# A hybrid decoder step on one core: sample attention in 32-column tiles, and one residual add moved in the FFN loops

## The chip, the cores and the metric

The kernel runs on one core of a Trainium2 chip, in one launch. The metric is the device time of that launch in microseconds (us); lower is better. The time given is the median of several runs, and one further execution was taken by the hardware profiler.

## What is computed

The reference is one inference step of a two-layer decoder trunk. 1024 prompt tokens and 8 samples of 4 new tokens each (32 rows) share all weights. Layer 0 mixes tokens with a gated short convolution, layer 1 with stick-breaking attention; each layer ends with a convolutional FFN of width 2816. Cut to what matters here:

```python
def stick_breaking(q, k, v, q_pos, k_pos, bias):
    z = einsum('bqhd,bkhd->bhqk', q, k) / sqrt(HEAD_DIM) + bias
    mask = k_pos < q_pos
    log_keep = where(mask, log_sigmoid(-z), 0)
    after = cumsum(log_keep, reverse=True) - log_keep
    w = where(mask, exp(log_sigmoid(z) + after), 0)
    return einsum('bhqk,bkhd->bqhd', w, v)

def conv_ffn(h, prev, w_up, w_dw, b_dw, w_down):
    g, u = split(h @ w_up, 2)
    gc, st = causal_dwconv(g, prev, w_dw)
    return (silu(gc + b_dw) * u) @ w_down, st
```

A sample's keys are 256 cached ones (two pages of 128) and its own new ones. There are 16 heads of 64, so the model width of 1024 is eight chunks of 128 features, and a chunk holds two heads.

## The kernel before, in words

All activations stay in SBUF, features on partitions and the 1056 tokens along the free axis in three blocks of 352. The large products are float32 split in three passes (`three`, lines 472 to 478): high part of the weights by high part of the activations, high by low, low by high. SyncE (SP) loads one raw weight tile after the other, GpSimd (POOL) splits it in `w_hi` and `w_lo`, TensorE (PE) multiplies, ScalarE (ACT) and VectorE (DVE) take the results out of PSUM. The order on every engine is written out by hand with semaphores; there is no planner.

**The FFN loop.** The 22 hidden chunks are worked in 11 pairs. After a first pair, five loop trips of two pairs each follow in each of the two layers, so 20 groups in all. A group is four up projections (gate and up of two chunks, `up`, `linear`) and then eight down tiles for the pair before (`down`, line 552). The results alternate between two PSUM areas `out[0]` and `out[1]`; `full[s]` tells that an area holds a result, `taken[s]` that it may be written again. In `down`, tile f waits for the area that tile f-2 has left (line 567). A down tile is 18 matmuls. DVE's `ffn_chunk` (line 1266) takes the gate (L1272), convolves it, scales it (L1279), multiplies with the up result straight from PSUM (L1283), waits until ACT has written `a_hi` (L948, in the rows the helper's line L836), and subtracts to get `a_lo` (L1285). After the second chunk's subtraction come the eight adds of the down tiles to the residual `x` (`add_x`, L1293), the one of tile 0 first. PE needs this group's `a_lo` only in the next group's down tiles (`a_ready`, line 565).

**Sample attention** stands between the prompt's attention and the output projection `wo`. It works on four pairs of samples, bp = 0 to 3. The 128 rows of a pair's scores are 2 samples of 64 rows, and these are 16 heads of 4 tokens. `q_rows` holds the queries as a stationary operand: for feature chunk c only the 8 columns of its two heads are nonzero. The steps of a pair:

- `sample_scores` (PE, line 761): 8 chunks by 2 samples, each a matmul of 64 stationary columns by 256 keys (L770), then 8 matmuls of 128 columns by the 32 new keys (L775) and a bf16 mask matmul (L777).
- `sample_sigmoids` (ACT, line 1092), `sample_weigh` (DVE, L1475 and L1477).
- `sample_turn` (PE, L784 and L785) and `sample_copy` (DVE, L1481 and L1482) turn the weights.
- `sample_values` (PE, line 788): 2 matmuls of 128 columns by 512 for the new values (L796), then 2 halves by 2 pages by 2 samples of 64 columns by 512 (L804). All 1024 features are computed for every head, in two PSUM banks `o_s`; a head's own 64 are picked at the end.
- `sample_rows` (ACT, line 1098) copies 128x1024 out of PSUM; `sample_out` (PE, L814) turns it in 8 transposes; `sample_take` (DVE, L1493) picks the heads' parts in 16 copies of 64x8 into `mixed`.

PE's order is `sample_scores(bp+1)`, `sample_out(bp-1)`, `sample_turn(bp)`, `sample_values(bp)`. The cached pages come by DMA from SP (lines 415 to 434): K and V of pairs 0 and 1 are loaded during the prompt's attention. Then K of pair 2 is issued once pair 0 is scored (line 424), V of pair 2 once pair 0's values are done (line 430), then SP reads the page numbers of pair 3 (line 419) and issues its K, and V of pair 3 follows once pair 1's values are done. A K or V load of a pair is four transfers of 512 KB. ACT reloads `x` (line 1090, 8 transfers of 528 KB) as the stage begins.

Of the kernel before, what the change touches and what calls it, by code (L numbers as in the profile page):

```python
# [21 lines left out]
P = 128  # L22
D = 1024
# [141 lines left out]
def build(nc, x_in, weights, taps_sc, taps_ffn, state_sc, state_ffn, gains, bias_heads, bias_rows,  # L165
# [6 lines left out]
    with ctx:  # L172
# [87 lines left out]

        q_rows = [sb(f"q_rows{n}", [P, KC * (P + 2 * NT)]) for n in range(2)]
        v_new = sb("v_new", [NS, D])
        o_rows = sb("o_rows", [P, D])
        beta_s = [sb(f"beta_s{n}", [P, PAST + NS]) for n in range(2)]
        keep_s = [sb(f"keep_s{n}", [P, PAST + NS]) for n in range(2)]
        prod_s = sb("prod_s", [P, PAST + NS])
# [17 lines left out]

        turned = [out[0][:, 2, :], out[1][:, 2, :]]
        attended = out[0][:, 1, :]
        o_s = out[0][:, 0:2, :].rearrange("p a b -> p (a b)")

        def sem(name):
            return ctx.enter_context(nc.semaphore(name))  # L290
# [180 lines left out]
        def _(pe):  # L471
# [289 lines left out]
            def sample_scores(bp):  # L761

                pe.wait_ge(s_set, bp + 1)
                bank_s = out[1][:, bp % 2, :]
                for b in range(2):
                    pe.wait_ge(page_k_in[2 * (bp % 2) + b], (bp // 2 + 1) * 32)
                for c in range(KC):
                    for b in range(2):
                        slot, rows = 2 * (bp % 2) + b, slice(64 * b, 64 * b + 64)
                        nc.tensor.matmul(bank_s[rows, 0:PAST], q_rows[bp % 2][:, c * P + 64 * b:c * P + 64 * b + 64],  # L770
                                         page_k[slot][:, c, :, :].rearrange("p g t -> p (g t)"),
                                         start=c == 0, stop=c == KC - 1, skip_group_check=True)

                for c in range(KC):
                    nc.tensor.matmul(bank_s[:, PAST:PAST + NS], q_rows[bp % 2][:, c * P:(c + 1) * P], k_s[:, c, :],  # L775
                                     start=c == 0, stop=False, skip_group_check=True)
                nc.tensor.matmul(bank_s[:, PAST:PAST + NS], ident_b[:, :], new_b[:, bp, :], start=False,  # L777
                                 stop=True, skip_group_check=True).then_inc(s_scored, 1)

# [8 lines left out]
            def sample_values(bp):  # L788

                pe.wait_ge(s_wt, bp + 1)  # L790

                if bp:
                    pe.wait_ge(s_o_rows, bp)

                for half in range(2):
                    nc.tensor.matmul(out[0][:, half, :], w_ts[0:NS, PAGES, :], v_new[:, 512 * half:512 * half + 512],  # L796
                                     start=True, stop=False, skip_group_check=True)
                for b in range(2):
                    pe.wait_ge(page_v_in[2 * (bp % 2) + b], (bp // 2 + 1) * 32)
                for half in range(2):  # L800
                    for g in range(PAGES):
                        for b in range(2):
                            slot, rows = 2 * (bp % 2) + b, slice(64 * b, 64 * b + 64)
                            mm = nc.tensor.matmul(out[0][rows, half, :], w_ts[:, g, rows],  # L804
                                                  page_v[slot][:, g, 512 * half:512 * half + 512], start=False,
                                                  stop=g == PAGES - 1, skip_group_check=True)
                mm.then_inc(s_full, 1)

            def sample_out(bp):
                pe.wait_ge(s_o_rows, bp + 1)  # L810

                pe.wait_ge(s_out, bp + 1)
                for c in range(KC):
                    mm = nc.tensor.transpose(score[1][:, c * P:(c + 1) * P], o_rows[:, c * P:(c + 1) * P], ident[:, :])  # L814
                mm.then_inc(s_o_turned, 1)

            sample_scores(0)
# [16 lines left out]
        def _(act):  # L834
# [262 lines left out]

            def sample_rows(bp):
                act.wait_ge(s_full, bp + 3)
                act_op(o_rows[:, :], o_s).then_inc(s_o_rows, 1)  # L1100

            sample_sigmoids(0)
            for bp in range(NB // 2):
# [23 lines left out]
        def _(dve):  # L1127
# [135 lines left out]
                        last.then_inc(tapped, 1)  # L1263
                last.then_inc(convolved, 1)

            def ffn_chunk(m, par, chunk, layer, k, trip, slot):
# [12 lines left out]
                V.tensor_tensor(y[par][:, :], y[par][:, :], rstd[:, :], ALU.mult).then_inc(y_scaled, 1)  # L1279
                dve.wait_ge(y_scaled, m + 1)  # L1280
                dve.wait_ge(full[s], trip * TRIP_FILLS + (FULL[name][s] + (k + 1) // 2 + 1))
                yy = wide(y[par][:, :])
                V.tensor_tensor(yy, yy, result(s), ALU.mult).then_inc(taken[s], 1)  # L1283
                dve.wait_ge(a_high, m - (KC - 1))
                V.tensor_tensor(a_lo[:, slot, par, :], y[par][:, :], a_hi[:, slot, par, :].bitcast(f32),  # L1285
                                ALU.subtract).then_inc(a_ready, 1)
# [8 lines left out]
            def ffn(layer):  # L1295
                name = f"ffn{layer}"
                m0 = M_FFN[layer]

                def up(m, chunk, k0, trip, slot):
                    for p in range(2):  # L1300
                        ffn_chunk(m + p, p, chunk + p, layer, k0 + 2 * p, trip, slot)

                def down(k0, trip):
                    for f in range(KC):
                        add_x(f, name, k0 + f, trip)

                up(m0, 0, 0, 0, 0)
                with dve.Fori(0, FFN_TRIPS) as i:
                    for n in range(2):
                        k0 = (4 + KC) * n + 4  # L1310
                        up(i * 4 + (m0 + 2 + 2 * n), i * 4 + (2 + 2 * n), k0, i, (n + 1) % 2)
                        down(k0 + 4, i)

            dve.wait_ge(gain_loaded, 16)
# [169 lines left out]
            def sample_take(bp):  # L1484

                dve.wait_ge(s_o_turned, bp + 1)
                for h in range(2):
                    rows = slice(DH * h, DH * h + DH)
                    o = mixed[rows, :, SEQ + bp * 2 * NT:SEQ + (bp + 1) * 2 * NT].rearrange("p c (b t) -> p c b t", b=2)

                    r = score[1][rows, :].rearrange("p (c b r) -> p c b r", c=KC, b=2)
                    for c in range(KC):
                        last = V.tensor_copy(o[:, c, :, :], r[:, c, :, 8 * c + 4 * h:8 * c + 4 * h + NT])  # L1493
                last.then_inc(s_out, 1)

            sample_q(0)
# [126 lines left out]
```

## Time and profile before

| | us |
|---|---|
| median of 3 runs | 2708.8 |
| lowest and highest | 2707.02 and 2710.52 |
| the profiled execution, its own time | 2711.09 |
| its span, first to last instruction | 2709.3 |
| PE busy with matmuls | 2609.6 |
| DVE busy | 1475.8 |
| POOL busy | 725.2 |
| ACT busy | 539.9 |

The time of an execution is its span and 1.8 us around it. Two records of the profile stand for each float32 matmul that isn't a transpose, because PE makes two passes; so 16 matmuls are "x32". In a form such as "128*64 128x256" the first pair is rows by stationary columns of the array, and the second is what streams through. "PEld" is the loading of the stationary operand, which runs beside PE's matmuls. The column "idle before" gives how long an engine had nothing to do and what ended that.

### The profile page before, as it was taken

To read this page: it belongs to the slowest core of one execution; us is meant where nothing else is said; L and a number is where in the kernel's file an instruction comes from. 1 tells how busy PE (TensorE), PEld (TensorE's weight loads), DVE (VectorE), ACT (ScalarE), POOL (GpSimd) and SP (SyncE) were. 2 spreads that over 40 slices of the span, in tenths; PEclk is the share of its full clock that TensorE was granted. 3 is DMA by queue.
4 is the path that set the end of the run, shared out by engine and by line. 5 is a ranking of instruction groups with operands and counts; after the bars stand their busy time and mean duration, and the time that the engine had idled before them with its cause. 6 is when DMAs were issued, how large, how long until landed. Compare 5 with 4: busy or idle time off the path is not lost.

```text
span 2709.3 us, 40755 instructions
## 1 busy us (share of the span) xinstructions
PE 2609.6 (96%) x16774; PEld 2472.5 (91%) x16774; DVE 1475.8 (54%) x1512; ACT 539.9 (20%) x1077; POOL 725.2 (27%) x415
## 2 busy tenths in 40 slices
PE   7999999999999999989999999789999999999996
PEld 7999999999999999988888888459999999999995
DVE  7333455444444455587777777533754444444446
ACT  4000221000000000144444444320300000000013
POOL 3333333223332233221111111013322233333333
PEclk9999999999999999999999999899999999999998
DMA  4111111111111111121111111631111111111111
GB/s 137 47 42 45 48 47 40 47 47 47 43 44 47 47 47 40 50 111 40 40 40 40 44 44 40 220 102 47 39 40 47 47 47 47 47 47 47 47 42 65
DMA packets 60330, 149.04 MB, mean 55 GB/s; under 512 B 5522, under 2 KB 28818, under 8 KB 60178
## 3 DMA queue, kind: packets, MB, share of 16 engines
q1 hardware_dynamic: 51298, 123.86, 14.2%
q10 hardware_dynamic: 8880, 22.85, 2.2%
q8 instruction: 132, 2.16, 0.3%
q14 instruction: 20, 0.16, 0.0%
HBM read 128.91 MB, written 17.78 MB: 54 GB/s over the span
## 4 chain that ended last, share of the span: by engine, by line
PE 86%; DVE 8%; issue 2%; ACT 2%; POOL 1%; DMA 0%; SPq 0%; DVEq 0%; POOLq 0%; ACTq 0%
PE bank L474 26%; PE bank L478 25%; PE bank L477 25%; PE bank L706 3%; PE bank L646 3%; PE bank L679 2%; DVE a_lo L1285 1%; DVE h_lo L1155 1%; DVE total L1164 1%; DVE x L1293 1%; DVE y L1283 1%; ACT a_hi L836 1%; POOL y_rows L466 1%; PE bank L770 1%; PE bank L804 1%
## 5 line engine op out<-in xcount | busy, mean ns | idle before, releaser
L474 PE MATMUL bank<-h_hi,w_hi 128*128 128x352 f32 x3648 | 1197.1, 328 | 29.8 <-DVE ext L1272 8.8
L478 PE MATMUL bank<-h_hi,w_lo 128*128 128x352 f32 x3648 | 1177.6, 323 | 0.0
L477 PE MATMUL bank<-h_lo,w_hi 128*128 128x352 f32 x3648 | 1176.6, 323 | 0.0
L450 POOL CAST w_hi<-raw 128x1024 fp32r<-128x1024 f32 x196 | 217.9, 1112 | 1937.7 <-PE bank L474 1894.3
L474 PEld LDWEIGHTS bank<-h_hi,w_hi 128*128 128x128 f32 x3648 | 690.2, 189 | 42.5 <-issue 31.2
L477 PEld LDWEIGHTS bank<-h_lo,w_hi 128*128 128x128 f32 x3648 | 691.7, 190 | 0.7 <-issue 0.4
L478 PEld LDWEIGHTS bank<-h_hi,w_lo 128*128 128x128 f32 x3648 | 691.3, 190 | 0.0
L452 POOL TENSOR_TENSOR w_lo<-raw,w_hi 128x1024 fp32r<-128x1024 f32 x196 | 488.1, 2490 | 15.7
L1293 DVE TENSOR_TENSOR x<-x,bank 128x1056 f32<-128x1056 f32 x174 | 216.2, 1251 | 290.8 <-PE bank L478 290.8
L474 PE MATMUL bank<-a_hi,w_hi 128*128 128x352 f32 x1056 | 343.9, 326 | 11.7 <-DVE x L1293 11.7
L477 PE MATMUL bank<-a_lo,w_hi 128*128 128x352 f32 x1056 | 342.1, 324 | 0.0
L478 PE MATMUL bank<-a_hi,w_lo 128*128 128x352 f32 x1056 | 341.1, 323 | 0.0
L1272 DVE TENSOR_TENSOR ext<-bank,rstd 128x1056 f32<-128x1056 f32 x44 | 55.4, 1259 | 333.7 <-PE bank L478 333.6
L474 PEld LDWEIGHTS bank<-a_hi,w_hi 128*128 128x128 f32 x1056 | 198.7, 188 | 20.1 <-DVE x L1293 16.3
L1405 DVE TENSOR_TENSOR_SCAN prod<-keep 128x895 f32<-128x895 f32 (+7 forms) x128 | 196.5, 1535 | 21.5 <-ACT keep L836 17.1
L836 ACT ACTIVATE smp<-ext 128x32 f32<-128x32 f32 x52 | 12.0, 231 | 949.3 <-DVE ext L1272 858.9
L477 PEld LDWEIGHTS bank<-a_lo,w_hi 128*128 128x128 f32 x1056 | 198.2, 188 | 0.2
L478 PEld LDWEIGHTS bank<-a_hi,w_lo 128*128 128x128 f32 x1056 | 198.3, 188 | 0.0
L836 ACT ACTIVATE beta<-bank,bias_pair 128x896 f32<-128x896 f32 (+7 forms) x128 | 94.9, 741 | 222.6 <-PE bank L649 218.6
L1285 DVE TENSOR_TENSOR a_lo<-y,a_hi 128x1056 fp32r<-128x1056 f32 x44 | 105.4, 2396 | 52.4 <-ACT a_hi L836 52.4
L1409 DVE TENSOR_TENSOR beta<-beta,prod 128x895 f32<-128x895 f32 (+7 forms) x128 | 125.3, 979 | 4.4
L1247 DVE TENSOR_SCALAR y<-ext,tap_ffn 128x1024 f32<-128x1024 f32 x44 | 116.3, 2643 | 9.7 <-DVE ext L1272 9.6
(111 smaller groups left out, 1757.7 us busy)
## 6 DMA issues: line engine op xcount, KB each, us to landing
raw<-weights SPq DMA_DIRECT2D x196, 512.0 KB, 3.4
page_k<-cache_k SPq DMA_DIRECT2D x16, 512.0 KB, 7.0
page_v<-cache_v SPq DMA_DIRECT2D x16, 512.0 KB, 6.1
x_spill<-x ACTq DMA_DIRECT2D x8, 528.0 KB, 6.1
k_out<-k_t ACTq DMA_DIRECT2D x8, 528.0 KB, 2.7
v_out<-v_t ACTq DMA_DIRECT2D x8, 528.0 KB, 2.9
x<-x_spill ACTq DMA_DIRECT2D x8, 528.0 KB, 7.4
y_out<-y_rows ACTq DMA_DIRECT2D x3, 1408.0 KB, 5.3
```

The source lines that it names most:

```text
L450: nc.gpsimd.tensor_copy(w_hi[ring][:, :], raw[slot][:, :]).then_inc(w_high, 1)
L452: nc.gpsimd.tensor_tensor(w_lo[ring][:, :], raw[slot][:, :], w_hi[ring][:, :].bitcast(f32), ALU.subtract).then_inc(w_split, 1)
L474: mm = nc.tensor.matmul(o, w_hi[w][:, c0:c0 + P], hi, start=first, stop=False)
L477: nc.tensor.matmul(o, w_hi[w][:, c0:c0 + P], lo, start=False, stop=False)
L478: return nc.tensor.matmul(o, w_lo[w][:, c0:c0 + P], hi, start=False, stop=last)
L646: nc.tensor.matmul(score[h][:, n0:n1], q_t[par][rows, i * P:(i + 1) * P], k_t[par][rows, n0:n1], start=True, stop=n1 < width)
L836: return nc.scalar.activation(o, i, func, **kw)
L1247: V.tensor_scalar(o[:, 0:SEQ], e[:, 0:SEQ], tap(0), None, ALU.mult).then_inc(tapped, 1)
L1285: V.tensor_tensor(a_lo[:, slot, par, :], y[par][:, :], a_hi[:, slot, par, :].bitcast(f32), ALU.subtract).then_inc(a_ready, 1)
L1293: V.tensor_tensor(xx, xx, result(s), ALU.add).then_inc(taken[s], 1)
L1405: V.tensor_tensor_scan(prod[:, width - 1:0:-1], back, back, 1.0, ALU.mult, ALU.bypass).then_inc(scanned, 1)
L1409: V.tensor_tensor(w[:, 0:width - 1], w[:, 0:width - 1], prod[:, 1:width], ALU.mult).then_inc(weighed, 1)
```

## The change

It has two parts. In sample attention the stationary operands shrink to 32 columns: each of the four quarters of the score rows (a sample's heads 0 to 7 or 8 to 15) takes only the four chunks that can be nonzero for it, and only its own half of the features of V. The output per pair is then 128x512 in one bank, so `o_rows` and `o_s` are two half-size buffers used in turn, the transposes go from 8 to 4 (into `spare`, one bank for each parity), and the picking copies from 16 of 64x8 to 8 of 64x16. The waits follow: values of bp wait for the row copy of bp-2, the row copy of bp for the transposes of bp-2, the transposes of bp for the picking of bp-2. In the FFN loops the add of down tile 0 moves ahead of the second chunk's last subtraction.

```diff
-        o_rows = sb("o_rows", [P, D])
+        o_rows = [sb(f"o_rows{n}", [P, D // 2]) for n in range(2)]
-        o_s = out[0][:, 0:2, :].rearrange("p a b -> p (a b)")
+        o_s = [out[0][:, n, :] for n in range(2)]
+        o_turned = [spare[:, n, :] for n in range(2)]
...
-                for c in range(KC):
+                for cc in range(KC // 2):
                     for b in range(2):
-                        slot, rows = 2 * (bp % 2) + b, slice(64 * b, 64 * b + 64)
-                        nc.tensor.matmul(bank_s[rows, 0:PAST], q_rows[bp % 2][:, c * P + 64 * b:c * P + 64 * b + 64],
-                                         page_k[slot][:, c, :, :].rearrange("p g t -> p (g t)"),
-                                         start=c == 0, stop=c == KC - 1, skip_group_check=True)
-
-                for c in range(KC):
-                    nc.tensor.matmul(bank_s[:, PAST:PAST + NS], q_rows[bp % 2][:, c * P:(c + 1) * P], k_s[:, c, :],
-                                     start=c == 0, stop=False, skip_group_check=True)
+                        for g in range(2):
+                            c, r = cc + g * KC // 2, 64 * b + 32 * g
+                            nc.tensor.matmul(bank_s[r:r + 32, 0:PAST], q_rows[bp % 2][:, c * P + r:c * P + r + 32],
+                                             page_k[2 * (bp % 2) + b][:, c, :, :].rearrange("p g t -> p (g t)"),
+                                             start=cc == 0, stop=cc == KC // 2 - 1, skip_group_check=True)
+
+                for cc in range(KC // 2):
+                    for b in range(2):
+                        for g in range(2):
+                            c, r = cc + g * KC // 2, 64 * b + 32 * g
+                            nc.tensor.matmul(bank_s[r:r + 32, PAST:PAST + NS], q_rows[bp % 2][:, c * P + r:c * P + r + 32],
+                                             k_s[:, c, :], start=cc == 0, stop=False, skip_group_check=True)
...
-                if bp:
-                    pe.wait_ge(s_o_rows, bp)
-
-                for half in range(2):
-                    nc.tensor.matmul(out[0][:, half, :], w_ts[0:NS, PAGES, :], v_new[:, 512 * half:512 * half + 512],
-                                     start=True, stop=False, skip_group_check=True)
+                if bp >= 2:
+                    pe.wait_ge(s_o_rows, bp - 1)
+
+                for r in range(0, P, 32):
+                    g = r // 32 % 2
+                    nc.tensor.matmul(o_s[bp % 2][r:r + 32, :], w_ts[0:NS, PAGES, r:r + 32],
+                                     v_new[:, 512 * g:512 * g + 512], start=True, stop=False, skip_group_check=True)
...
-                for half in range(2):
-                    for g in range(PAGES):
-                        for b in range(2):
+                for page in range(PAGES):
+                    for r in range(0, P, 32):
+                        b, g = r // 64, r // 32 % 2
+                        mm = nc.tensor.matmul(o_s[bp % 2][r:r + 32, :], w_ts[:, page, r:r + 32],
+                                              page_v[2 * (bp % 2) + b][:, page, 512 * g:512 * g + 512], start=False,
+                                              stop=page == PAGES - 1, skip_group_check=True)
...
-                pe.wait_ge(s_out, bp + 1)
-                for c in range(KC):
-                    mm = nc.tensor.transpose(score[1][:, c * P:(c + 1) * P], o_rows[:, c * P:(c + 1) * P], ident[:, :])
+                pe.wait_ge(s_out, max(bp, 1))
+                for cc in range(KC // 2):
+                    mm = nc.tensor.transpose(o_turned[bp % 2][:, cc * P:(cc + 1) * P],
+                                             o_rows[bp % 2][:, cc * P:(cc + 1) * P], ident[:, :])
...
                 act.wait_ge(s_full, bp + 3)
-                act_op(o_rows[:, :], o_s).then_inc(s_o_rows, 1)
+                if bp >= 2:
+                    act.wait_ge(s_o_turned, bp - 1)
+                act_op(o_rows[bp % 2][:, :], o_s[bp % 2]).then_inc(s_o_rows, 1)
...
                 V.tensor_tensor(yy, yy, result(s), ALU.mult).then_inc(taken[s], 1)
+                if between is not None:
+                    between()
                 dve.wait_ge(a_high, m - (KC - 1))
...
                 def down(k0, trip):
-                    for f in range(KC):
+                    for f in range(1, KC):
                         add_x(f, name, k0 + f, trip)
...
-                        up(i * 4 + (m0 + 2 + 2 * n), i * 4 + (2 + 2 * n), k0, i, (n + 1) % 2)
+                        up(i * 4 + (m0 + 2 + 2 * n), i * 4 + (2 + 2 * n), k0, i, (n + 1) % 2,
+                           lambda: add_x(0, name, k0 + 4, i))
                         down(k0 + 4, i)
...
-                    for c in range(KC):
-                        last = V.tensor_copy(o[:, c, :, :], r[:, c, :, 8 * c + 4 * h:8 * c + 4 * h + NT])
+                    for c in range(KC // 2):
+                        last = V.tensor_copy(o[:, c, :, :, :], r[:, c, :, :, 8 * c + 4 * h:8 * c + 4 * h + NT])
```

`between` runs for the second chunk of a group only (`between if p else None`).

## Rows read from the trace of the kernel before

**Rows 1.** The page: span, busy time of the engines, chain that ended last.

```profile
span 2709.3 us, 40755 instructions
...
PE 2609.6 (96%) x16774; PEld 2472.5 (91%) x16774; DVE 1475.8 (54%) x1512; ACT 539.9 (20%) x1077; POOL 725.2 (27%) x415
...
PE 86%; DVE 8%; issue 2%; ACT 2%; POOL 1%; DMA 0%; SPq 0%; DVEq 0%; POOLq 0%; ACTq 0%
```

**Rows 2.** Waits of PE, 425 to 1145 us (layer 0's FFN): total us, times, longest.

```profile
PE bank L474 <- DVE x L1293: 4.3, 10, 0.4
```

**Rows 3.** Waits of PE, 1930 to 2660 us (layer 1's FFN).

```profile
PE bank L474 <- DVE x L1293: 5.8, 11, 1.5
```

**Rows 4.** Timeline of DVE, 2005 to 2012 us: start, us, instructions, idle before.

```profile
2005.46 1.25 DVE L1283 TENSOR_TENSOR y<-y,bank 128x1056 f32<-128x1056 f32 x1 [1.63 <-PE bank L478]
2007.87 2.52 DVE L1285 TENSOR_TENSOR a_lo<-y,a_hi 128x1056 fp32r<-128x1056 f32 x1 [1.16 <-ACT a_hi L836]
2010.31 2.40 DVE L1293 TENSOR_TENSOR x<-x,bank 128x1056 f32<-128x1056 f32 x2
```

**Rows 5.** Timeline of PE, 2010.5 to 2011.7 us.

```profile
2010.70 0.32 PE L477 MATMUL bank<-a_lo,w_hi 128*128 128x352 f32 x1
2010.86 0.32 PE L478 MATMUL bank<-a_hi,w_lo 128*128 128x352 f32 x1
2011.61 0.43 PE L474 MATMUL bank<-a_hi,w_hi 128*128 128x352 f32 x1 [0.42 <-DVE x L1293]
```

**Rows 6.** Timeline of PE, 1740 to 1809.2 us (sample attention).

```profile
1740.95 5.50 PE L770 MATMUL bank<-page_k,q_rows 128*64 128x256 f32 x32 [0.31 <-DVE q_rows L1465]
...
1763.67 3.62 PE L770 MATMUL bank<-page_k,q_rows 128*64 128x256 f32 x32
1767.22 1.97 PE L775 MATMUL bank<-k_s,q_rows 128*128 128x32 f32 x16
...
1771.16 1.98 PE L796 MATMUL bank<-v_new,w_ts 32*128 32x512 f32 x4 [0.70 <-DVE w_ts L1482]
1773.07 3.65 PE L804 MATMUL bank<-page_v,w_ts 128*64 128x512 f32 x16
1778.85 5.33 PE L770 MATMUL bank<-page_k,q_rows 128*64 128x256 f32 x32 [2.12 <-DMA page_k<-cache_k]
...
1785.95 1.07 PE L814 MATMUL bank<-ident,o_rows 128*128 128x128 f32 x8
...
1798.77 5.35 PE L804 MATMUL bank<-page_v,w_ts 128*64 128x512 f32 x16
...
1809.11 0.40 PE L474 MATMUL bank<-h_hi,w_hi 128*128 128x352 f32 x1 [2.78 <-DVE h_lo L1241]
```

**Rows 7.** Timeline of PE's weight loads, 1732.8 to 1734.3 us (prompt attention).

```profile
1732.84 0.64 PEld L706 LDWEIGHTS bank<-w_first,v_rows 128*64 128x64 f32 x12 [1.58 <-ACT w_first L836]
```

**Rows 8.** Windows of sample attention; last three columns: granted clock, DMA share, GB/s.

```profile
1740.00:1757.50 17.50, 16.49 (x108) 10.51 (x106) 5.77 (x14) 1.78 (x4) 0.00 (x0) 0.79 1.05 352
1753.70:1763.90 10.20, 9.50 (x30) 3.15 (x31) 2.12 (x6) 0.90 (x3) 0.00 (x0) 0.67 0.45 112
1763.90:1783.80 19.90, 17.07 (x111) 9.94 (x108) 3.45 (x22) 2.93 (x4) 0.00 (x0) 0.91 0.97 316
```

**Rows 9.** Timeline of SP's DMA issues, 1690 to 1830 us.

```profile
1763.89 1.78 SPq L433 DMA_DIRECT2D page_v<-cache_v  x4
1768.53 4.82 SPq L427 DMA_DIRECT2D page_k<-cache_k  x4
1776.77 1.77 SPq L433 DMA_DIRECT2D page_v<-cache_v  x4
```

**Rows 10.** Timeline of ACT, 1755 to 1809 us (the row copies).

```profile
1804.16 1.02 ACT L836 ACTIVATE o_rows<-bank 128x1024 f32<-128x1024 f32 x1 [9.48 <-PE bank L804]
```

**Rows 11.** Groups of ACT, 1690 to 1740 us: busy us, mean ns, idle before.

```profile
L836 ACT ACTIVATE mixed<-bank 128x512 f32<-128x512 f32 x3 | 1.8, 602 | 5.0 <-PE bank L706 5.0
```

**Rows 12.** Timeline of DVE, 1803 to 1808 us (the picking copies).

```profile
1806.37 1.43 DVE L1493 COPY mixed<-bank 64x8 f32<-64x8 f32 x16 [8.22 <-PE bank L814]
```

More of the change, by code:

```diff
@@ L790, in sample_values @@
                 pe.wait_ge(s_wt, bp + 1)
-                if bp:
-                    pe.wait_ge(s_o_rows, bp)
-                for half in range(2):
-                    nc.tensor.matmul(out[0][:, half, :], w_ts[0:NS, PAGES, :], v_new[:, 512 * half:512 * half + 512],
-                                     start=True, stop=False, skip_group_check=True)
+                if bp >= 2:
[4 more added lines that the diff above has]
+                                     v_new[:, 512 * g:512 * g + 512], start=True, stop=False, skip_group_check=True)
                 for b in range(2):
                     pe.wait_ge(page_v_in[2 * (bp % 2) + b], (bp // 2 + 1) * 32)
-                for half in range(2):
-                    for g in range(PAGES):
-                        for b in range(2):
[L803 to L806, printed above, removed]
+                for page in range(PAGES):
[4 more added lines that the diff above has]
+                                              stop=page == PAGES - 1, skip_group_check=True)
                 mm.then_inc(s_full, 1)
@@ L1264, in conv, with ffn_chunk @@
                 last.then_inc(convolved, 1)
-            def ffn_chunk(m, par, chunk, layer, k, trip, slot):
+            def ffn_chunk(m, par, chunk, layer, k, trip, slot, between=None):
                 name = f"ffn{layer}"
@@ L1297, in ffn, with up @@
                 m0 = M_FFN[layer]
-                def up(m, chunk, k0, trip, slot):
+                def up(m, chunk, k0, trip, slot, between=None):
                     for p in range(2):
-                        ffn_chunk(m + p, p, chunk + p, layer, k0 + 2 * p, trip, slot)
+                        ffn_chunk(m + p, p, chunk + p, layer, k0 + 2 * p, trip, slot, between if p else None)
                 def down(k0, trip):
-                    for f in range(KC):
+                    for f in range(1, KC):
                         add_x(f, name, k0 + f, trip)
@@ L1488, in sample_take @@
                     rows = slice(DH * h, DH * h + DH)
-                    o = mixed[rows, :, SEQ + bp * 2 * NT:SEQ + (bp + 1) * 2 * NT].rearrange("p c (b t) -> p c b t", b=2)
-                    r = score[1][rows, :].rearrange("p (c b r) -> p c b r", c=KC, b=2)
-                    for c in range(KC):
-                        last = V.tensor_copy(o[:, c, :, :], r[:, c, :, 8 * c + 4 * h:8 * c + 4 * h + NT])
+                    o = mixed[rows, :, SEQ + bp * 2 * NT:SEQ + (bp + 1) * 2 * NT].rearrange("p (g c) (b t) -> p c b g t", g=2, b=2)
+                    r = o_turned[bp % 2][rows, :].rearrange("p (c b g r) -> p c b g r", c=KC // 2, b=2, g=2)
+                    for c in range(KC // 2):
+                        last = V.tensor_copy(o[:, c, :, :, :], r[:, c, :, :, 8 * c + 4 * h:8 * c + 4 * h + NT])
                 last.then_inc(s_out, 1)
```

## The prediction, made before the changed kernel was run

> **What bounds the kernel now.** I read the page first: PE is busy for 96% of the span and carries 86% of the chain that ended last [rows 1]. So only what shortens PE's stream, or a wait in it, can count. The waits of PE over each layer's FFN come next: 10 waits for the residual add in one layer and 11 in the other, all but one at most 0.4 us long [rows 2, 3]. There are 10 groups a layer, so every group of the FFN loop has one. The timelines of DVE and PE around one show why. The last up tile ends at 2005.4; DVE multiplies, waits for ACT, subtracts until 2010.3, and only then adds down tile 0, until 2011.56 [rows 4]. PE starts a matmul every 0.16 us, but after the one at 2010.86 the next starts at 2011.61 [rows 5]: down tile 2 needs the area that this add sets free.
>
> The third reading is PE's timeline of sample attention, from the first score matmul at 1740.95 to the first matmul of `wo` at 1809.11, 68.2 us [rows 6]. PE is not the only bound there. For pair 3 it waits 2.1 us for pages [rows 6], and the windows show the DMA engines saturated from 1740 to 1757.5 (share 1.05, 352 GB/s), and nearly so from 1763.9 to 1783.8 (0.97, 316 GB/s) [rows 8]. The same matmuls also take longer in places: 32 records of L770 took 5.50 and 5.33 us at two places and 3.62 at a third, and 16 of L804 took 5.35 instead of 3.65 [rows 6]. From 1753.7 to 1763.9 the granted clock was 0.67 [rows 8], a mixture of 1.2 and 2.4 GHz, after PE had waited for the turned weights.
>
> **The FFN part.** Nothing is added or removed; one add of 1.25 us (2.40 for two) passes one subtraction of 2.5 us [rows 4]. The stall costs 0.75 - 0.16 = 0.59 us [rows 5], and 20 x 0.59 = **11.8 us**. What is late next? A down tile is 18 matmuls of 0.16, 2.9 us. In the example group tile 0 ends at 2005.4 + 2.9 = 2008.3. DVE's wait for it now stands ahead of the subtraction; DVE had been idle until 2007.87 anyway [rows 4]. The add ends at 2009.6, well before tile 2 is due at 2011.2; the subtraction ends at 2012.1, the add of tile 1 at 2013.4, and tile 3 is due at 2014.1. So 0.7 us is left. Queued behind the moved wait are only DVE's own subtraction and adds; PE needs `a_lo` in the next group, four up tiles later. No DMA issue or other queue is passed. Bounds: 11.8 if the cover holds; were each group 0.7 + 0.2 us later, 20 x 0.2 = 4 us of it would come back. I take 11.8.
>
> **The sample part, PE's work for a pair.** Matmuls of 64 columns in different halves of the array already overlap: 32 records of 256 columns take 3.55 us to the next line's start, 0.22 for two [rows 6], and 512 columns take 3.70 us for 16 records, 0.46 for two (to the issue at 1776.77 that their end releases [rows 6, 9]). If four quarters overlap as two halves do:
> - L770: still 32 records, now four at a time, 8 x 0.22 = 1.8 us, down 1.8.
> - L775: 16 records of 128 columns take 1.8 us (0.11 each); 32 records of 32 columns replace them. No row has such loads in a stream. The nearest is the 12 loads of 64 columns in 0.64 us, 0.05 each [rows 7], which gives 32 x 0.05 = 1.7. I take no change; the bounds are half of it (-0.9) and one 0.11 for each (+1.8).
> - L796: 4 records in turn take 1.91 us [rows 6]; 8, four at a time, 0.95.
> - L804: 16 records, four at a time, 4 x 0.46 = 1.85, down 1.85. The values together go from 5.6 to 2.8.
> - L814: 4 transposes instead of 8 in 1.07 [rows 6], down 0.45. The row copy halves, 1.02 [rows 10] to the 0.60 of a 128x512 copy [rows 11]. Picking: 8 copies instead of 16 in 1.43, 0.09 each [rows 12], down 0.7; doubling 8 columns to 16 is costed at nothing.
>
> L770's new form needs a weight load and a matmul every 0.22 / 4 = 0.055 us, just what rows 7 show, so that is where it may fall short. The new waits reach back two pairs, and what they wait for ended a whole pair ago; they cost nothing.
>
> **Where it stays on the path.** Most of the saved time of pairs 0 to 2 meets the page loads.
> - K of pair 2 shares saturated engines with the reload of `x`; an earlier issue doesn't bring its end ahead of 1757.5 [rows 8]. The scores of pair 2 started at 1763.67 [rows 6]. By the terms above pairs 0 and 1 are scored by about 1750 and values(0) ends at 1754 (at full clock) to 1757 (at half). So PE waits here, up to 3 us.
> - V of pair 2 is then issued at about 1755.5 instead of 1763.89 [rows 9]. K of pair 3 is issued 4.6 us behind it (1768.53 [rows 9]), and landed 15.0 behind it (1778.85 [rows 6]): 1770.5. By the rate, from 1757.5 on 4.2 MB at 316 GB/s [rows 8] end at 1770.8. I take 1770.8, between 1769 and 1772: **8.0 us** earlier than before.
> - From there PE's chain runs to the end, and V of pair 3 is in by about 1777, ahead of its use. Scores(3) start after a wait and were slow before (7.1 us from 1778.85 to 1785.95 [rows 6]); with half the clock for four quarters 3.6 + 1.8, down 1.7. Then two rounds of values: 2.8 for pair 2, and 3.0 for pair 3, where 5.35 [rows 6] shows the lower clock (I take a mixture again). Three rounds of transposes, 3 x 0.45; two row copies, 2 x 0.4; the last picking, 0.7. Together 1.7 + 2.8 + 3.0 + 1.35 + 0.8 + 0.7 = **10.3 us**.
>
> Sum: 8.0 + 10.3 = 18.3 for the stage, with 11.8 for the FFNs 30.1 us. The profiled execution took 2711.09 us, so it would take 2681.0; that execution lies 2.3 above the median of 2708.8, so the median forecast is **2678.7 us**. The bounds of the stage: if every round after K of pair 3 runs at the lower clock and the pages land at 1772, the gain is 18.3 - 2.8 - 1.3 - 1.2 = 13; if all run at the upper, pages land at 1769 and L775 halves, 18.3 + 1.8 + 1.3 + 0.9 = 22. I give the forecast 2674 to 2684.
>
> The Trainium skill ("TensorE: Matmul & The Clock Gate", section on packing small matmuls) puts three column tiles at 2.38 times one, not 3 times. By that, an estimate, a group of four would take 1.26 times a single one, some 2 us more over the last chain, and the time would be near 2681. The same skill ("TensorEngine Tiling (Array Packing)", Instruction Overhead) warns against tiling where a dimension is already small, which speaks against the new L775 with its 32 streamed columns; no run here shows its charge yet.
>
> **The rivals.**
> 1. *Quarters overlap only two at a time*, or loads and issue hold L770 to 0.11 us a record as L775's loads do. For: no row shows four. Against: two halves overlap in full. Then scores and values keep their length, L775 costs up to 1.8 more, and of the stage only the transposes, copies and picking stay, about 3 us, less about one L775 round of 1.8: 2708.8 - 11.8 - 1 = **2696**. Chance 0.13.
> 2. *Quarters run one after another* (the slower side). The place is PE's L770, L796 and L804: (32 x 0.22) + (24 x 0.46) = 18.1 us a pair against 9.2, plus 8.9 - 0.85 = 8.0, four times 32; the page waits give about 3 back, the FFN part 11.8. That is 2708.8 + 17 = **2726**. It decides below about 1.3 quarters at a time, where the stage's loss passes 11.8. Against it stand the overlapping halves. Chance 0.04.
> 3. *The FFN stall only moves*: the subtraction now stands behind the add, and tile 3 waits for the add of tile 1. For: only 0.7 us of cover, and the subtraction's length depends on POOL's work beside it. Against: it would need nearly 1 us more. Price: 4 to 12 us back, **2687** in the middle. Chance 0.06.
> 4. *The page loads take back more*: with PE idle twice, pair after pair runs at the lower clock, and the stage gives 11 instead of 18: **2686**. Chance 0.09.
>
> **The chances.** The forecast has 0.68; the rivals 0.13, 0.04, 0.06 and 0.09. The range holds forecast, rivals 3 and 4 and the optimistic end: 2673 to 2692, 0.83 in all. A measurement of this kernel tells 0.2% (5.4 us) from no change. Only rival 2 is slower: slower 0.05; same 0.03, for two rivals meeting; faster 0.92.
>
> **What would show it.** In the changed profile: no wait of PE for L1293 in the 20 groups, DVE's order multiply, add, subtract; 32 records of L770 in about 1.9 us at full clock and 16 of L804 in 1.9; scores(2) starting near 1757.5 and scores(3) near 1771, both released by pages; the first matmul of `wo` near 1791. If L770 still takes 3.6 us, quarters don't overlap and the sum for the stage falls; if the stage ends near 1791 but the total doesn't follow, the FFN part is wrong.

## The result, and the profile after

The changed kernel takes 2683.9 us (median of 4 runs, 2680.5 to 2688.8) against 2707.9 for the kernel before (4 runs): a ratio of 0.991, 95% interval 0.989 to 0.993, so 24.0 us less. The forecast was 2678.7, 29 us less than the same median. The profiled execution took 2683.9 us, 27.2 less than that of before.

The page of the changed kernel, its first lines and its chain of waits:

```profile
span 2682.1 us, 40852 instructions
...
PE 2582.4 (96%) x16838; PEld 2461.6 (92%) x16838; DVE 1450.8 (54%) x1480; ACT 537.9 (20%) x1077; POOL 724.8 (27%) x415
...
PE 90%; DVE 5%; issue 2%; ACT 1%; SPq 1%; POOL 1%; DMA 1%; POOLq 0%; DVEq 0%; ACTq 0%
```

PE's share of the chain rose from 86 to 90% and DVE's fell from 8 to 5% [rows 1]: the 20 pieces of the chain that ran through a multiply, ACT's copy, a subtraction and an add are gone. PE's waits from 425 to 1150 us, layer 0's FFN:

```profile
PE bank L475 <- DVE x L1303: 1.5, 1, 1.5
```

and DVE's timeline in a group of layer 1:

```profile
1983.03 1.25 DVE L1291 TENSOR_TENSOR y<-y,bank 128x1056 f32<-128x1056 f32 x1 [1.70 <-PE bank L479]
1985.91 1.25 DVE L1303 TENSOR_TENSOR x<-x,bank 128x1056 f32<-128x1056 f32 x1 [1.62 <-PE bank L479]
1987.08 1.25 DVE L1295 TENSOR_TENSOR a_lo<-y,a_hi 128x1056 fp32r<-128x1056 f32 x1
1988.79 1.25 DVE L1303 TENSOR_TENSOR x<-x,bank 128x1056 f32<-128x1056 f32 x1 [0.46 <-PE bank L479]
```

The ten waits of [rows 2] are gone; the one that is left is the 1.5 us one outside the groups, which [rows 3] had too. The order is as forecast: multiply, add, subtract, add. The subtraction takes 1.25 us in its new place, not the 2.5 of [rows 4], so DVE is ahead of its work: it stands idle for 0.46 us before the add of tile 1.

PE's timeline of sample attention, which answers to [rows 6]:

```profile
1735.84 3.34 PE L772 MATMUL bank<-page_k,q_rows 128*32 128x256 f32 x32 [1.14 <-DVE q_rows L1476]
1739.01 0.48 PE L780 MATMUL bank<-k_s,q_rows 128*32 128x32 f32 x32
1739.54 1.93 PE L772 MATMUL bank<-page_k,q_rows 128*32 128x256 f32 x32
...
1743.20 1.06 PE L802 MATMUL bank<-v_new,w_ts 32*32 32x512 f32 x8 [0.70 <-DVE w_ts L1493]
1744.19 1.92 PE L809 MATMUL bank<-page_v,w_ts 128*32 128x512 f32 x16
1754.65 3.64 PE L772 MATMUL bank<-page_k,q_rows 128*32 128x256 f32 x32 [8.54 <-DMA page_k<-cache_k]
...
1767.00 3.64 PE L772 MATMUL bank<-page_k,q_rows 128*32 128x256 f32 x32 [3.48 <-DMA page_k<-cache_k]
...
1779.83 3.53 PE L809 MATMUL bank<-page_v,w_ts 128*32 128x512 f32 x16
1784.09 0.66 PE L819 MATMUL bank<-ident,o_rows 128*128 128x128 f32 x4 [0.73 <-ACT o_rows L842]
1786.95 0.63 PE L475 MATMUL bank<-h_hi,w_hi 128*128 128x352 f32 x1 [2.21 <-DVE h_lo L1249]
```

Four quarters stream at a time without loss: 32 records of L772 in 1.93 us where two halves took 3.62, and 16 of L809 in 1.92 instead of 3.65. The new keys (L780) fell from 1.97 to 0.48. From the first score matmul to the first of `wo` the stage takes 1786.95 - 1735.84 = 51.1 us, where it took 68.2. And PE now waits 12.0 us for pages, 8.5 and 3.5, where it waited 2.1. SP's issues show what the loads do now:

```profile
1739.80 9.37 SPq L428 DMA_DIRECT2D page_k<-cache_k  x4
1749.26 3.10 SPq L434 DMA_DIRECT2D page_v<-cache_v  x4
1755.28 6.69 SPq L428 DMA_DIRECT2D page_k<-cache_k  x4
```

The columns of the table are worked from the timelines of the profiled executions, in us. "K2" and "K3" are the starts of the scores of pairs 2 and 3 after the first score matmul; "FFN 1 to end" runs from the first matmul of `wo` to the end of the span.

| kernel | K2 | K3 | stage | FFN 1 to end |
|---|---|---|---|---|
| before | 22.7 | 37.9 | 68.2 | 900.2 |
| changed | 18.8 | 31.2 | 51.1 | 895.1 |
| forecast | 16.6 | 29.9 | 49.9 | |
| e1_ffn_only | 19.0 | 33.9 | 64.2 | 896.1 |
| e2_sample_only | 18.4 | 31.2 | 51.2 | 901.3 |
| e3_quarters_in_turn | 18.0 | 31.3 | 52.6 | 897.5 |
| e7_before_x_late | 19.1 | 33.9 | 64.2 | 899.9 |
| e4_x_late | 14.5 | 27.6 | 44.6 | 895.1 |
| e5_k_first | 19.0 | 27.6 | 43.2 | 894.1 |
| e6_both | 14.8 | 24.0 | 41.3 | 894.6 |
| e9_order_filled | 15.4 | 22.8 | 38.7 | 895.3 |
| e11_v_after_k | 18.5 | 33.2 | 50.7 | 895.8 |

### The profile page after: what moved, and what is told of

It is laid out like the page before. It is cut to its first block, busy times and chain, and to the rows that moved or that the text cites. A ratio compares the mean times of both kernels' runs of the same rounds, so it can differ in the third digit from the quotient of the medians.

```text
span 2682.1 us, 40852 instructions
## 1 busy us (share of the span) xinstructions
PE 2582.4 (96%) x16838; PEld 2461.6 (92%) x16838; DVE 1450.8 (54%) x1480; ACT 537.9 (20%) x1077; POOL 724.8 (27%) x415
## 4 chain that ended last, share of the span: by engine, by line
PE 90%; DVE 5%; issue 2%; ACT 1%; SPq 1%; POOL 1%; DMA 1%; POOLq 0%; DVEq 0%; ACTq 0%
PE bank L475 27%; PE bank L479 27%; PE bank L478 27%; PE bank L707 3%; PE bank L647 3%; PE bank L680 2%; DVE total L1172 1%; DVE h_lo L1163 1%; POOL y_rows L467 1%; SPq L428 1%; PE bank L650 0%; DVE h_lo L1249 0%; DVE x L1221 0%; DMA x<-x_in 0%; ACT beta L842 0%
## 5 line engine op out<-in xcount | busy, mean ns | idle before, releaser
L453 POOL TENSOR_TENSOR w_lo<-raw,w_hi 128x1024 fp32r<-128x1024 f32 x196 | 488.3, 2491 | 15.7
L1262 DVE SCALAR_TENSOR_TENSOR y<-ext,tap_ffn,y 128x1024 f32<-128x1024 f32 x88 | 113.0, 1284 | 0.0
```

Source lines behind the costliest of these rows:

```text
L453: nc.gpsimd.tensor_tensor(w_lo[ring][:, :], raw[slot][:, :], w_hi[ring][:, :].bitcast(f32), ALU.subtract).then_inc(w_split, 1)
L1262: main = V.scalar_tensor_tensor(o[:, 0:SEQ], e[:, n:n + SEQ], tap(n), o[:, 0:SEQ], ALU.mult, ALU.add)
```

## The experiments

Each ratio below is against runs of the kernel before made beside that experiment. Differences to the changed kernel are differences of medians from different rounds, so where they are small the intervals of the ratios and the lengths of the stage say more.

**One part at a time.** First the kernel before with the moved add alone; the edit is the FFN part of the diff above.

> The kernel before with the moved add alone. Theory (20 stalls of 0.59 us go, nothing takes their place): 11.8 us less than before, near 2696, PE waits for the residual add only once or twice in the FFN loops. Rival (the stall moves to down tile 3, or PE waits elsewhere): 0 to 8 us less. In the changed kernel's trace the two FFN loops gave back about 6.3 and 5.0 us, so 10 to 12 is expected.

Measured: 2696.1 us, ratio 0.996 (0.995 to 0.998), 12.3 us less than the kernel before. Its waits of PE from 425 to 2650 us have one line for the residual add:

```profile
PE bank L474 <- DVE x L1295: 3.1, 2, 1.5
```

Twice 1.5 us, one in each layer's FFN and both outside the groups. The stall went and nothing took its place.

Then the other part alone:

```diff
-                    for f in range(1, KC):
+                    for f in range(KC):
...
-                        up(i * 4 + (m0 + 2 + 2 * n), i * 4 + (2 + 2 * n), k0, i, (n + 1) % 2,
-                           lambda: add_x(0, name, k0 + 4, i))
+                        up(i * 4 + (m0 + 2 + 2 * n), i * 4 + (2 + 2 * n), k0, i, (n + 1) % 2)
```

> The changed kernel with the residual adds in their old place: the sample part alone. Theory (the two parts lie in different stretches and add up): the stage takes 51 us instead of 68, so 17 us less than before, near 2691, and 20 stalls of PE on the residual add are back. Rival (the parts are not additive, or the stage's length depends on how the run falls): 12 to 14 us less, which with 11.8 for the other part would give the 24 that were measured for both.

Measured: 2694.9 us, ratio 0.995 (0.994 to 0.996), 13.5 us less. Its waits of PE over the same stretch:

```profile
PE bank L772 <- DMA page_k<-cache_k: 11.8, 2, 8.1
PE bank L475 <- DVE x L1303: 11.6, 22, 1.5
```

The 20 stalls are back. 12.3 and 13.5 make 25.8, and both together gave 24.0, within the scatter of these medians: the parts add up. But the sample part is worth 13.5 us, not 17 (my expectation) nor 18.3 (the forecast), although the stage takes 51.2 us in this trace as in the changed kernel's. The table has the reason. The stage of before took 68.2 us in the one execution that I had, and 64.2 in the two others with the same stage, e1_ffn_only and e7_before_x_late. PE's timeline of e1_ffn_only:

```profile
1750.28 3.65 PE L804 MATMUL bank<-page_v,w_ts 128*64 128x512 f32 x16
...
1768.64 3.67 PE L770 MATMUL bank<-page_k,q_rows 128*64 128x256 f32 x32 [1.82 <-DMA page_k<-cache_k]
```

For the first of these two places [rows 8] had a clock of 0.67, and the trace of before has there:

```profile
1754.97 3.77 PE L796 MATMUL bank<-v_new,w_ts 32*128 32x512 f32 x4 [0.70 <-DVE w_ts L1482]
1758.67 5.17 PE L804 MATMUL bank<-page_v,w_ts 128*64 128x512 f32 x16
```

This is where most of the 4 us lie: the scores of pair 2 start at 22.7 there and at 19.0 here. The second place, 5.33 us in [rows 6], makes no difference in the sum, since e1_ffn_only pays as much at the values of pair 2; from the scores of pair 3 to `wo` both traces take 30.3 us. Whether PE falls to 1.2 GHz at a given place differs between executions of the same stage, and mine was a slow one. 64.2 - 51.2 = 13.0 is what this part is worth against the other two executions: 2.7 us from the earlier scores of pair 3 (33.9 and 31.2) and 10.3 from what follows them (30.3 and 20.0).

**Do quarters need neighbours?** The loops of the scores, new keys and cached values were swapped, so that one quarter's matmuls come in a row:

```diff
-                for cc in range(KC // 2):
-                    for b in range(2):
-                        for g in range(2):
+                for b in range(2):
+                    for g in range(2):
+                        for cc in range(KC // 2):
...
-                for page in range(PAGES):
-                    for r in range(0, P, 32):
+                for r in range(0, P, 32):
+                    for page in range(PAGES):
```

> The changed kernel with the same matmuls, but all of one quarter of the columns before the next quarter's (scores, new keys, cached values). Theory (the gain is that four quarters stream at a time, and this needs neighbours in different quarters): 32 score records take about 32 x 0.21 = 6.8 us instead of 1.75, the 16 of the cached values 6.8 instead of 1.8, together some 10 us more for each pair, 30 us or more over the stage after the page waits give some back: 2710 to 2720. Rival (the gain is only that columns of zeros are dropped, or the engine overlaps quarters over any distance): within 4 us of the changed kernel.

Measured: 2688.8 us, ratio 0.992 (0.991 to 0.994), 5 us more than the changed kernel by the medians, with overlapping intervals, and not 30; the stage is 1.5 us longer. PE's timeline of this kernel from 1745.7 to 1754.8 us:

```profile
1745.78 3.95 PE L772 MATMUL bank<-page_k,q_rows 128*32 128x256 f32 x29
1749.35 0.40 PE L780 MATMUL bank<-k_s,q_rows 128*32 128x32 f32 x8
1749.56 0.38 PE L772 MATMUL bank<-page_k,q_rows 128*32 128x256 f32 x1
1749.56 0.41 PE L780 MATMUL bank<-k_s,q_rows 128*32 128x32 f32 x12
1749.78 0.38 PE L772 MATMUL bank<-page_k,q_rows 128*32 128x256 f32 x1
...
1752.81 1.94 PE L809 MATMUL bank<-page_v,w_ts 128*32 128x512 f32 x16
```

The cached values, 4 records in a row for each quarter, overlap in full (1.94). The scores, 8 in a row, overlap in part: 3.57 us to the first new key where neighbours take 1.75. New-key records start ahead of the last score records, though the program has them behind: quarters run on independently, over some distance. The Trainium skill says that matmuls start and end in program order ("TensorE: Matmul & The Clock Gate", section on packing small matmuls); the starts in this trace are not in that order. So neither theory held. The expectation's 30 us fell, and the rival's "over any distance" did too. From the first score record to the end of the new keys PE lost 2.6 us a pair (for pair 1, 4.8 us instead of 2.2), and for the pairs ahead of the page loads the wait took it back: 2.60 us of wait before pair 2 instead of 8.54.

**The pages.** What bounds the stage now? The reload of `x` moved from ACT at the stage's start to SP, behind the last page:

```diff
-            for f in range(KC):
-                act.dma_start(x[:, f, :], x_spill[f, :, :]).then_inc(x_back, 16)
...
+            sp.wait_ge(x_spilled, 16 * KC)
+            for f in range(KC):
+                sp.dma_start(x[:, f, :], x_spill[f, :, :]).then_inc(x_back, 16)
             rest = N_TILES - early
```

> The changed kernel with the reload of x (4.3 MB) issued by SP after the last pages, instead of by ACT at the stage's start. Theory (K of pair 2 came 18.8 us after the first score matmul because it shared the DMA engines with x): K of pair 2 lands about 7 us earlier, and K of pair 3 with it by 4 to 7 us; x is back before the first tile of the output projection is added: 4 to 7 us less than the changed kernel, near 2678. Rival (the page loads are slow by themselves, through their small pieces or SP's issue): no change.

Measured: 2678.8 us, ratio 0.989 (0.988 to 0.991), 5.1 less than the changed kernel, though the intervals overlap; the stage takes 44.6 us instead of 51.1. K of pair 2 came 4.4 us earlier, K of pair 3 3.5, and the chain behind it took 17.0 us instead of 20.0, for a reason that the part on the clock gives. The same edit on the kernel before:

> The kernel before with the late reload of x. Theory (the pages came in time before, but for about 2 us, and became the bound only through the faster matmuls): at most 2 us less than before, 2706 to 2709. Rival (the share that x takes of the DMA engines held up the kernel before too): 4 us less or more.

Measured: 2706.7 us, ratio 0.9997 (0.9987 to 1.0007). Nothing, and its stage takes 64.2 us as in e1_ffn_only. So the bound by page loads is one that the faster matmuls uncovered.

Then the order of SP's issues, K of pair 3 ahead of V of pair 2, with the page numbers read first; the loop is unrolled, and its second half becomes:

```diff
+            ids2, ids3 = pages_of(2), pages_of(3)
+            load_k(2, ids2)
+            load_k(3, ids3)
+            load_v(2, ids2)
+            load_v(3, ids3)
```

> The changed kernel with K of pair 3 issued before V of pair 2, and the page numbers of both read ahead of the waits (PE needs this K first). Theory (the stage hangs on the landing of K of pair 3, 31.2 us after the first score matmul, because its issue stands behind V of pair 2 in SP's queue): K of pair 3 lands near 27 us, V of pair 2 then becomes the wait at 33: 2 to 4 us less than the changed kernel, 2680 to 2682. Rival (only the bytes count, the order doesn't): no change.

Measured: 2675.2 us, ratio 0.987 (0.986 to 0.989), 8.7 less than the changed kernel, more than the 2 to 4 that I expected: V of pair 2 did not become the wait. All that PE waits for in this stage:

```profile
PE bank L780 <- DMA page_k<-cache_k: 8.8, 1, 8.8
PE bank L810 <- DVE w_ts L1501: 2.8, 4, 0.7
PE bank L483 <- DVE h_lo L1257: 2.2, 1, 2.2
PE bank L827 <- ACT o_rows L850: 1.4, 2, 0.7
PE bank L780 <- DVE q_rows L1484: 1.2, 1, 1.2
```

K of pair 3 is there when PE comes for it. The stage is 7.9 us shorter than the changed kernel's (43.2 and 51.1). Only 3.6 of them are the earlier start of the scores of pair 3. The other 4.3 lie behind it: with no wait before these scores, PE's chain to `wo` takes 15.7 us instead of 20.0. The window of this kernel over the beginning of that chain has the full clock, with the DMA engines as busy as in the changed kernel (columns as in [rows 8]):

```profile
1765.00:1770.00 5.00, 4.30 (x80) 2.10 (x76) 2.50 (x12) 0.89 (x2) 0.00 (x0) 1.00 0.99 384
```

Both edits together:

> The order of e5_k_first together with the late reload of x of e4_x_late. Theory (page loads are the bound, x takes a share of the DMA engines, and the order puts the wrong load first): K of pair 2 lands 14.5 us after the first score matmul, K of pair 3 near 20, V near 26 and 32, the stage takes 38 to 40 us instead of 44.6 in e4_x_late: near 2673. Rival (PE's own chain and its low clock after waits bound the stage by now): 42 to 44 us, 2676 to 2679.

Measured: 2671.9 us, ratio 0.986 (0.985 to 0.988). The stage of the profiled execution takes 41.3 us, between the theory and the rival; that execution, at 2677.6, was the slowest of its four.

**When did K of pair 2 land?** The forecast had it 16.6 us after the first score matmul, and it was 18.8.

```diff
                     sp.wait_ge(s_full, i * 2 + (pair + 1))
+                    for n in (2 * pair, 2 * pair + 1):
+                        sp.wait_ge(page_k_in[n], i * 32 + 32)
```

> The changed kernel, V of each pair issued only when K of the same pair has landed. Theory (K of pair 2 landed 2.2 us later than forecast because V of pair 2 was by then issued early enough to take a share of the DMA engines): K of pair 2 lands 16.5 to 17 us after the first score matmul instead of 18.8; K of pair 3 is issued later, so the stage is no shorter: 2683 to 2687. Rival (K of pair 2 is slow through the reload of x alone): it still lands at 18.8, and the stage grows by 2 us or more.

Measured: 2684.4 us, ratio 0.991 (0.989 to 0.992), as the changed kernel; K of pair 2 still let PE go only at 18.5, so my theory fell. The windows of this kernel show what I had misread:

```profile
1752.40:1754.40 2.00, 0.00 (x0) 0.00 (x0) 0.00 (x0) 0.00 (x0) 0.00 (x0) 0.53 1.18 287
1754.40:1756.40 2.00, 0.00 (x0) 0.00 (x0) 0.00 (x0) 0.00 (x0) 0.00 (x0) 0.50 0.95 234
1756.40:1757.80 1.40, 0.00 (x0) 0.00 (x0) 0.00 (x0) 0.00 (x0) 0.00 (x0) 0.50 0.05 14
```

The first score matmul is at 1739.3 here. The bulk of the bytes is through by 1756.4, 17.1 us after it and near the forecast's 16.6, but PE starts at 1757.84. A trickle of small packets runs on behind the bulk (the 0.05 of the last window), and the last of the four transfers, issued at 1750.6, lands 7.1 us later, at 1757.7: PE starts 0.1 us behind that. The trace of before had the same tail. There the last transfer of K of pair 2 was issued at 1752.1 and landed 7.4 us later, at 1759.5, which is 18.5 us after the first score matmul and 2.0 us after the 1757.5 at which the forecast had it. Nothing waited for it there, so it stood in no list of waits. The rival's rise of the stage by 2 us didn't come either; K of pair 3 came 2.0 later, and PE's chain behind it took 17.5 us instead of 20.0, its last values at the full clock (1.92 us instead of 3.53).

**The clock after a wait.** PE's waits for pages were filled with matmuls that feed nothing:

```diff
+                for n in range({2: 16, 3: 7}.get(bp, 0)):
+                    nc.tensor.matmul(out[0][0:P, 2, 0:512], ident[:, :], mixed[:, n % KC, 0:512],
+                                     start=True, stop=True, skip_group_check=True)
                 for b in range(2):
                     pe.wait_ge(page_k_in[2 * (bp % 2) + b], (bp // 2 + 1) * 32)
```

> The changed kernel with 16 and 7 float32 matmuls of 128 columns by 512 that feed nothing, placed where PE waits for K of pairs 2 and 3 (6.8 and 3.0 us of work at the full clock, in waits of 8.5 and 3.5). Theory (scores, transposes and new keys of pairs 2 and 3 take twice as long because the clock falls while PE waits): scores of both pairs take 1.9 us instead of 3.6 and the stage ends 2 to 4 us earlier; only what follows K of pair 3 counts: near 2681. Rival (the clock falls for another reason, or the filling delays the real work by as much): no change or up to 3 us more.

Measured: 2687.8 us, ratio 0.992 (0.991 to 0.993). I had sized the filling wrong: a float32 matmul is two records, so 16 took not 6.8 but 14.0 us. The timeline of PE:

```profile
1745.98 14.00 PE L767 MATMUL bank<-mixed,ident 128*128 128x512 f32 x32
...
1772.82 1.93 PE L775 MATMUL bank<-page_k,q_rows 128*32 128x256 f32 x32
...
1788.51 0.40 PE L475 MATMUL bank<-h_hi,w_hi 128*128 128x352 f32 x1 [2.21 <-DVE h_lo L1252]
```

It overran both waits, and the stage grew by only 2 us, because the chain from the scores of pair 3 to `wo` now took 1788.51 - 1772.82 = 15.7 us where it took 1786.95 - 1767.00 = 20.0. The windows of the two kernels over their chains show the clock. Kernel with the filling:

```profile
1772.80:1788.50 15.70, 10.66 (x132) 4.43 (x132) 5.47 (x34) 3.34 (x8) 0.00 (x0) 1.00 0.04 17
```

and the changed kernel, its wait for K of pair 2, the scores behind it, the scores of pair 3, and the last values:

```profile
1746.10:1754.60 8.50, 0.01 (x2) 0.00 (x0) 0.00 (x0) 0.60 (x1) 0.00 (x0) 0.67 1.14 316
1754.60:1758.60 4.00, 3.95 (x64) 2.40 (x64) 0.00 (x0) 0.00 (x0) 0.00 (x0) 0.50 1.02 394
...
1767.00:1771.00 4.00, 4.00 (x64) 2.31 (x65) 0.00 (x0) 0.00 (x0) 0.00 (x0) 0.50 0.98 363
1778.80:1783.50 4.70, 4.56 (x24) 0.75 (x24) 0.72 (x8) 0.06 (x1) 0.00 (x0) 0.64 0.00 0
```

So 4.3 us of the changed kernel's chain hang on the clock. The DMA engines were idle over the chain of e8_filled and not in the changed kernel; that they aren't the cause is shown by e5_k_first, whose chain took the same 15.7 us beside page loads. A filling of the right length was to collect them, 9 and 3 matmuls instead of 16 and 7:

> The changed kernel with 9 and 3 matmuls that feed nothing (7.7 and 2.6 us) in PE's waits of 8.5 and 3.5 us for K of pairs 2 and 3, in place of the 14.0 and 6.3 us of e8_filled, which overran them. Theory (clock): from the landing of K of pair 3 to the output projection PE's chain took 20.0 us in the changed kernel and 15.7 in e8_filled; with the filling inside the waits the stage ends about 4 us earlier, near 2680. Rival: the filling delays K of pair 3 or its scores, no change.

Measured: 2681.9 us, ratio 0.989 (0.988 to 0.991), 2 less than the changed kernel, with overlapping intervals. In the profiled execution K of pair 3 came late, at 32.1 us, PE stood idle for 4.0 us behind the filling, and the scores took 3.64 us again. So this is inconclusive.

On top of e6_both, 4 such matmuls before the scores of pair 2 (the same edit with other numbers), and then 2 more before `wo`:

> The kernel of e6_both with 4 matmuls that feed nothing (0.85 us each at the full clock, as e8_filled showed: 16 took 14.0) in PE's 4.3 us wait for K of pair 2. Theory (what is left of the stage is PE's chain, and half of it runs at the lower clock after this wait): scores of pair 2 take 1.9 us instead of 3.6 and what follows is faster too, 3 to 5 us less than e6_both, near 2668. Rival (the chain is bound by the waits between engines, not by the clock): within 1 us of e6_both.

> e9_order_filled with 2 more such matmuls in PE's 2.2 us wait before the output projection. Theory (the output projection starts at the lower clock in some runs, its first ten matmuls 0.3 us each instead of 0.16): up to 1.3 us less than e9_order_filled. Rival (the projection's start is bound by VectorE's low halves): the same as e9_order_filled.

Measured: 2671.9 us, ratio 0.987 (0.985 to 0.988), and 2674.4 us, ratio 0.987 (0.986 to 0.989). The scores of pairs 2 and 3 took 1.93 or 1.94 us in both traces and the stages 38.7 and 38.3 us, the shortest of all; the medians are no better than e6_both's 2671.9. That fits executions of e6_both that keep the clock without help, but its only trace is of one that didn't, so this wasn't shown. Before `wo` the filling let the first matmul start at 1777.45 at full speed, but 5 us of spread between executions covers 1 us of gain.

e6_both and e9_order_filled beat both kernels of the study by 12 us and more; their intervals (up to 0.988) lie below that of the change (from 0.989).

## Why the prediction was right, point by point

- **The FFN part held.** 20 x 0.59 = 11.8 us was forecast, 12.3 measured alone, with PE's waits gone as said. Rival 3, a stall that only moves, is refuted; the cover was even thicker, since the subtraction takes half as long in its new place. The forecast's 2.5 us for it was the length beside an operation of POOL (see the last section).
- **Four quarters at a time held** (1.93 and 1.92 us, or 1.75 from the first score record to the first new key; forecast 1.8 and 1.85), and with it rivals 1 and 2 fell. The estimate from the Trainium skill's 2.38 for three column tiles (the same page and section as above) would give 1.26 x 1.8 = 2.3 us for L772; the trace has 1.93, so nothing of that loss shows. Its warning against tiling a small dimension ("TensorEngine Tiling (Array Packing)", Instruction Overhead) does not come true for L780.
- **The new keys were mis-sized on the good side.** I took no change, with half as the lower bound. The 32 records start 0.013 us apart and take 0.48 instead of 1.97. Only pair 3's lie behind the last page wait, and there it brought 1.2 us (0.6 instead of 1.8 from their first record to the mask).
- **The page waits came where they were said to be**, before pairs 2 and 3, but the step "K of pair 2 lands at 1757.5" failed by 2.2 us: the end of the saturated stretch was taken for the landing. In the trace of before itself this K landed at 1759.5, 18.5 us after the first score matmul; in the changed kernel its scores start at 18.8. That an earlier issue doesn't bring the landing forward was right. K of pair 3 came at 31.2 instead of 29.9, and the late K of pair 2 accounts for it: 12.4 us lie between the two, where 13.3 were forecast.
- **The chain behind K of pair 3** was forecast at 20.0 us and took 20.0, but not by its terms: the scores with new keys took 4.05 instead of 5.4, and the lower clock made transposes (1.09 for the first four) and the last values (3.53, forecast 3.0) longer. The wait for a row copy fell from 1.12 to 0.73, the wait before `wo` from 2.78 to 2.21, near the 0.4 and 0.7 forecast.
- **The sum** in the profiled pair: 30.1 forecast, 27.2 measured. 1.3 of the 2.9 missing are K of pair 3, 0.3 the FFN loops, and the rest lies ahead of the first FFN group, where this execution was 1.3 us later.
- **The median** fell short by another 3 us (24.0), and here the step that failed is how the base was used: I took the whole stage of the profiled execution, 68.2 us, as that of the median. Two other executions of that stage took 64.2. That the profiled run was 2.3 us over the median was seen, and only carried along, not looked for in the stretch that the change touches. The optimistic half of the range, and the size of rival 4, would have been set otherwise. The number is in part luck: over medians the sample part gave 13.5 us where 18.3 was forecast, and 2683.9 lies nearer to rival 4's 2686 than to 2678.7. Rival 4's mechanism is there too, since PE waited twice and ran the scores behind both waits at the lower clock (0.50); the lower clock cost 4.3 us of the last chain, and the forecast had taken a mixture of the two clocks there.

## What to carry to other kernels

When PE's part of a stage shrinks by half, list the DMA issues behind it in the order in which PE will want the data, before costing any matmul: here a change of that order (K before V, with the page numbers read ahead) was worth 8.7 us, over a third of what the whole change had brought, about half of it because PE no longer waited and kept its clock. Take the landing of a load from its issue and the time to landing, and not from the end of the busy stretch of the DMA engines. Read a stage's length in more than one execution where the clock dips inside it, because the dip comes and goes. And look for an add whose input lies finished behind an operation that still waits for another engine: moving it ahead was worth 12.3 us here, nearly as much as re-tiling the attention (13.5).

## What the runs showed of the hardware that wasn't expected

- Quarters of 32 columns progress independently of each other, also where the program doesn't interleave them: 16 records with 4 in a row per quarter took 1.94 us, as with neighbours, and 32 with 8 in a row took 3.57 instead of 1.75.
- 32 records with loads of 32 columns and 32 streamed columns started in 0.41 us, 0.013 us each, in four quarters.
- DVE's subtraction of `a_lo`, both inputs in SBUF, made almost no headway while POOL was splitting a weight tile. Lines of the kernel before:

```profile
2053.62 2.41 POOL L452 TENSOR_TENSOR w_lo<-raw,w_hi 128x1024 fp32r<-128x1024 f32 x1
2054.76 2.38 DVE L1285 TENSOR_TENSOR a_lo<-y,a_hi 128x1056 fp32r<-128x1056 f32 x1 [1.23 <-ACT a_hi L836]
```

  They overlap for 1.27 us, and the subtraction ends 1.11 us after POOL does. All 132 subtractions in the traces of the kernel before, the changed one and e1_ffn_only follow this: the 46 that no POOL work overlaps take 1.25 or 1.26 us, six of them in the old place right behind ACT's copy, and the 86 others take their overlap with L452 and 1.10 to 1.13 us more. In its new place the second chunk's subtraction starts after POOL has finished. An add of a down tile, with one input in PSUM, took 1.25 us beside the same work of POOL (at 1985.91). No run changed POOL's work, so this rests on the traces' timing alone.
- SP's issue of four K loads took 9.4 us when it fell into the reload of `x`, 4.8 us without it (e4_x_late), and behind it in SP's order V of pair 2 was issued 3.0 us later and K of pair 3 4.4 us later, counted from the first score matmul. That full queues hold the issue up is my reading; no run tested it by itself.
